# Four tokens instead of two side by side in the one-hot tiles of a product-key selection

## The reference

```
q   = (xt @ w_query).reshape(t, 8, 2, 128)
sc  = einsum('thpd,hpnd->thpn', q, sub_keys)
s1, i1 = top_k(sc[:, :, 0], 16);  s2, i2 = top_k(sc[:, :, 1], 16)
cand = s1[..., :, None] + s2[..., None, :]          # 16 x 16 candidates a head
top_s, ci = top_k(cand, 16)
experts = i1[ci // 16] * 128 + i2[ci % 16]          # 8 heads x 16 = 128 experts a token
gate = softmax(top_s)
act  = gelu(einsum('thkd,td->thk', u_tab[experts], xb))
y    = einsum('thk,thkd->td', gate * act, v_tab[experts])
```

## Time and profile before

| | value |
|---|---|
| median of three executions | 3107.72 us |
| profiled execution, its own time | 3113.7 us |
| its span, first to last instruction | 3111.9 us |
| TensorE busy over the span | 2840.0 us (91%) |
| VectorE busy | 2122.1 us (68%) |
| ScalarE busy | 1109.1 us (36%) |
| GpSimd busy | 1756.4 us (56%) |
| octets on the time axis | from 1344 to 1863 us |

### The profile page before, as it was taken

The page is one execution under the profiler, slowest core; times in us unless marked ns, Lnnn a source line. Parts: engine busy times, 40 slices in busy tenths (PEclk is TensorE's granted clock), DMA queues, the critical chain, the costliest instruction groups (busy, mean ns, idle before and its releaser), DMA issues. The chain is left out here.

```text
span 3111.9 us, 47231 instructions
## 1 busy us (share of the span) xinstructions
PE 2840.0 (91%) x15880; PEld 1549.7 (50%) x15880; DVE 2122.1 (68%) x3995; ACT 1109.1 (36%) x1480; POOL 1756.4 (56%) x1614
## 2 busy tenths in 40 slices
PE   6998788899999999988999999589999998999998
PEld 3444763455555555555666665334444443444443
DVE  2498974311667777767787874367778776877877
ACT  4332344122344444445666663212212221221212
POOL 1312553011244344455666667588888887888884
PEclk8999887999999999999999999899999999999999
DMA  3200002011233333357778777889999998999995
GB/s 114 77 24 21 0 30 113 28 40 40 80 112 113 108 116 106 118 200 262 281 274 296 269 285 272 268 314 359 338 365 352 342 366 289 341 350 364 331 353 225
DMA packets 260396, 648.60 MB, mean 208 GB/s; under 512 B 16992, under 2 KB 115552, under 8 KB 257136
## 3 DMA queue, kind: packets, MB, share of 16 engines
q1 hardware_dynamic: 186176, 378.33, 34.2%
q0 software_dynamic: 74160, 269.52, 23.5%
HBM read 542.39 MB, written 105.91 MB: 208 GB/s over the span
## 5 line engine op out<-in xcount | busy, mean ns | idle before, releaser
L91 POOL TENSOR_TENSOR w_low<-w_ring,w_high 128x1024 f16<-128x1024 f32 x164 | 385.6, 2352 | 976.6 <-ACT w_ring L86 976.5
L1247 PE MATMUL psum<-region_y,w_high 128*128 128x384 f16 x2048 | 675.5, 330 | 20.6 <-POOL w_low L91 19.0
L1667 PE MATMUL psum<-vh,wh 128*128 128x512 bf16 x1536 | 585.3, 381 | 100.0 <-POOL wl L1716 64.1
L1248 PE MATMUL psum<-region_y,w_high 128*128 128x384 f16 x2048 | 674.8, 329 | 0.0
L1249 PE MATMUL psum<-region_y,w_low 128*128 128x384 f16 x2048 | 674.3, 329 | 0.0
L1668 PE MATMUL psum<-vl,wh 128*128 128x512 bf16 x1536 | 585.1, 381 | 0.0
L1669 PE MATMUL psum<-vh,wl 128*128 128x512 bf16 x1536 | 584.4, 380 | 0.0
L1683 ACT ACTIVATE vh<-w_ring 128x1024 bf16<-128x1024 f32 x128 | 135.1, 1055 | 823.2 <-DMA w_ring<-in_v_t_dram 778.3
L1811 DVE TENSOR_TENSOR region_x<-region_x,psum 128x1024 f32<-128x1024 f32 x192 | 233.9, 1218 | 148.6 <-PE psum L1669 148.2
L1711 POOL TENSOR_TENSOR vl<-w_ring,vh 128x1024 bf16<-128x1024 f32 x128 | 273.3, 2136 | 49.5 <-ACT vh L1683 47.5
L1667 PEld LDWEIGHTS psum<-vh,wh 128*128 128x128 bf16 x1536 | 150.8, 98 | 298.6 <-issue 63.3
(11 more groups left out here) (236 smaller groups left out, 4882.4 us busy)
## 6 DMA issues: line engine op xcount, KB each, us to landing
w_ring<-in_u_t_dram SPq DMA_DIRECT2D x128, 512.0 KB, 4.1
w_ring<-in_v_t_dram SPq DMA_DIRECT2D x128, 512.0 KB, 6.6
acts_dram<-ge SPq DMA_DIRECT2D x128, 384.0 KB, 2.5
gates_dram<-scores SPq DMA_DIRECT2D x24, 2048.0 KB, 8.9
gt<-gates_dram SPq DMA_DIRECT2D x32, 1536.0 KB, 13.6
at<-acts_dram SPq DMA_DIRECT2D x32, 1536.0 KB, 21.1
w_ring<-in_w_stream_dram SPq DMA_DIRECT2D x20, 512.0 KB, 3.2
w_ring<-in_w_q_dram SPq DMA_DIRECT2D x16, 512.0 KB, 3.2
```

The lines of the kernel that those rows point to most:

```text
L91: pool.tensor_tensor(self.wl[:, s, :], self.wf[:, s, :], self.wh[:, s, :], ALU.subtract).then_inc(self.w_lo, 1)
L1247: pe.matmul(a, uh[:, par, row], xh[:, n, cols], start=(n == 0), stop=False)
L1248: pe.matmul(a, uh[:, par, row], xl[:, n, cols], start=False, stop=False)
L1667: pe.matmul(a, wh[:, par, c, rows], vh[:, par, c, cols], start=(c == 0), stop=False)
```

## The change

The tile `hot` gets another order of elements. Four tokens are neighbours instead of two, and two such groups make the octet instead of four pairs. The planes, the number of instructions, their sizes in elements, the waits and the buffers stay. VectorE still writes 1024 elements in one run, but reads its second operand in runs of four bf16 values (8 bytes) that repeat 128 times, instead of runs of two (4 bytes). The iota tile is 512 instead of 256 elements. TensorE reads the matrix of a token at every fourth bf16 value, a step of 8 bytes instead of 4, for the stationary and for the moving operand.

```diff
-    LANES = 2
     QUAD = OCT // 2
-    ROWS = OCT // LANES
@@
     hot = flat[...].bitcast(BF16).rearrange(
-        "p (r n q i t) -> p r n q i t", r=2, n=4, q=ROWS, i=P)
+        "p (r n q i t) -> p r n q i t", r=2, n=4, q=2, i=P)
@@
-    iota_2 = flat[:, at:at + P * LANES // 2].bitcast(BF16).rearrange("p (q i t) -> p q i t", q=1, t=LANES)
+    iota_4 = flat[:, at:at + P * QUAD // 2].bitcast(BF16).rearrange("p (q i t) -> p q i t", q=1, t=QUAD)
@@ octet on TensorE
-                        q, lane = divmod(QUAD * b + t, LANES)
                         for part in (2, 3):
-                            last = pe.matmul(psum[:, 4 + 2 * r + b, t * P:(t + 1) * P], hot[:, r, 0, q, :, lane],
-                                             hot[:, r, part, q, :, lane], start=(part == 2), stop=(part == 3))
+                            last = pe.matmul(psum[:, 4 + 2 * r + b, t * P:(t + 1) * P], hot[:, r, 0, b, :, t],
+                                             hot[:, r, part, b, :, t], start=(part == 2), stop=(part == 3))
@@ octet on VectorE
-                    return ap.rearrange("p (q a t) -> p q a t", q=ROWS, a=1).to_broadcast([P, ROWS, P, LANES])
-
-                iota = iota_2.to_broadcast([P, ROWS, P, LANES])
+                    return ap.rearrange("p (q a t) -> p q a t", q=2, a=1).to_broadcast([P, 2, P, QUAD])
+
+                iota = iota_4.to_broadcast([P, 2, P, QUAD])
@@ once, ahead of the octets
-            dve.tensor_copy(iota_2.rearrange("p q i t -> p (q i) t"), iota_x[:, :, 0:LANES])
+            dve.tensor_copy(iota_4.rearrange("p q i t -> p (q i) t"), iota_x[:, :, 0:QUAD])
```

## The result

The changed kernel takes 3144.35 us (median of four, 3141.85 to 3149.72), the kernel before beside it 3110.71 us (3107.39 to 3115.12): a ratio of 1.0102, 95% interval 1.0088 to 1.0116. It is 34 us slower. The forecast was 3154, its likeliest case 3135 to 3189.

The account below looks back on a forecast made before the run. TensorE was taken to pace the octets: 52.5 ns more a matmul makes 81 us over 96 octets, less 35 us absorbed by waits, so +46 on 3107.7 gives 3154 us. The 8-in-10 range was 3103 to 3185 us.

Parts of the forecast that it names:

- TensorE sets the pace of the stretch: Octets, slices 18 to 24: TensorE, busy 479.0 of 516.1 us, bounds the stretch from first to last octet.
- The 53 us, 41.6 of waits and 11 of low clock: Octets' stretch: 516 us less 463 of TensorE work leaves 53, waits for VectorE and matmuls at the lower clock.
- VectorE is not changed: VectorE's four octet instructions stay at 0.60 us each, as they already stream at twice the float32 rate.
- The rule weighed there: Skill's rule for VectorE: full rate only in runs of two or more adjacent 4-byte words, so 8-byte runs would gain.
- A matmul costs 110 ns: TensorE's octet matmuls at a step of 8 bytes: 110 ns instead of 57.5, 81 us over 96 octets.
- The bracket [57.5, 112] of the rows: Bounds in ns for an octet matmul: the 4-byte step's price below, float32 matmuls at full clock above.
- Two thirds of the waits absorb, 35 us: TensorE's waits and low clock in the octets, 53 us, take up 35 of the 81 us added.
- The sum: Whole kernel: 81 us more of TensorE less 35 absorbed gives +46 us, 3154 us from 3107.7.
- The step costs nothing: Rival on TensorE's octet reads: 8 bytes apart is still full rate, time 3108 us, give or take 4; chance 33%.
- A partial cost, because only one operand is slowed: Rival on TensorE's octet matmuls: 65 to 85 ns each, 3114 to 3129 us; chance 13%.
- faster: Rival on VectorE: 8-byte runs remove its fixed 0.06 us or some long instructions, 3098 us in the middle; chance 7%.
- would stay: Said under the rival of a slower VectorE (2%): stretched octet instructions, 2.62 us beside GpSimd's work, remain.

Follow-up runs that it names:

- lanes1: The kernel before with one token to a run: TensorE reads both operands contiguously, VectorE's second operand has inner step 0; 3248.8 us beside 3100.9.
- move32: The kernel before with the moving operand alone read at a step of 32 bytes instead of 4; 3387.7 us beside 3100.9.
- mov8: The kernel before with the moving operand's planes alone at a step of 8 bytes, the stationary one kept at 4; 3141.6 us, ratio 1.0088.
- rows_later_quad: The changed kernel with VectorE's two gathered rows of a slot taken one octet later; 3142.6 us, ratio 1.0110 to the kernel before.

## Why the prediction was right, point by point

- **TensorE sets the pace of the stretch.** Right; the stretch grew by 38 us, and nothing behind it took any back beyond what executions differ by.
- **The 53 us, 41.6 of waits and 11 of low clock.** The sum is right and its parts are not. The 41.6 us hold the wait of 4.73 us ahead of the first octet, which is no part of the stretch. Inside it TensorE idled 37 us (516.10 - 479.04), and the low clock had 16. The forecast uses only the 53, so it did not move.
- **VectorE is not changed.** Right: a median of 684 ns before and 683 after. The rule weighed there, by which it would have gained, finds nothing here to gain, and lanes1 shows that the limit lies between runs of one value and of two.
- **A matmul costs 110 ns.** Measured 116 to 118, so the term is 90 us and not 81. The bracket [57.5, 112] of the rows was passed slightly, and the step to it was loose: 9 to 10 bytes a ns make 102 to 114 ns, not 107 to 115. The way to it (9 to 10 bytes crossed in a ns) gave the right size from a wrong law, which is luck in part: up to 16 bytes the two laws give the same price, but at 32 bytes the engine crosses 17.7 bytes a ns (4096 in 231 ns). What it had right is that the step of 4 stands at the edge of what is free.
- **Two thirds of the waits absorb, 35 us.** This was the mis-sized term: 90 - 38 = 52 us, the whole of the 53 that the stretch had above 463. The prediction held back a part because TensorE would also delay its suppliers. It does (VectorE waits for it 83.5 us), but VectorE and the rows have 1.9 us a slot more, and TensorE waits for them nowhere in the stretch.
- **The sum.** +46 forecast, +34 timed. The errors, 9 us too little and 17 too much, partly cancel, and give 38 us, the growth of the stretch; the 4 us to the timed 34 are within what executions differ by.
- **The rivals.** "The step costs nothing" falls with the first octet, for the moving operand; it was right for the stationary one. "A partial cost, because only one operand is slowed" had the operand right and the rate wrong. For "faster" the long octet instructions did go, by their timing against GpSimd and not by the 8-byte runs (move32, with 4-byte runs, has none either); no time was gained by it, as TensorE sets the pace. That they "would stay", as the prediction had it under another rival, was wrong.

## What to carry to other kernels

A layout that is read across by TensorE as the moving operand should, by these runs on bf16, put at least four of its columns into each 16 bytes. That is a step of 4 bytes, and each step beyond costs in proportion up to 16. The stationary operand may be laid out more widely while its load is hidden behind matmuls: at 8 bytes it cost 2 to 3 us over 1536 of them. A cost that is added to the pacing engine first eats that engine's own waits, so weigh it against the stretch with its waits taken away: the 34 us seen here were 72 once another order of instructions had removed most of them.

## What was not expected of the hardware

- The clock fell in a TensorE that never idled. At steps of 16 and 32 bytes the granted clock was 0.90 over 807 and 804 us, at 8 bytes 1.00. No idle time in the profile points to it.
- A matmul that its moving operand's read paces takes as long at half the clock: 16 of them 1.85 us in mov8 at 0.50 granted and at 1.00, where at a step of 4 bytes they take 1.69 and 0.92.
- A slower matmul can leave the kernel no slower. With a step of 6 bytes TensorE has 96 x 0.47 = 45 us more to do, but the stretch took 507 us instead of 515 and the single run 3093.0 beside 3100.9. That is 96 x (3.90 + 1.39) = 508, the stretch without waits: TensorE was busy 506.7 of 508.7 us at a granted clock of 1.00. The run lies below every execution of the kernel before on record (the lowest 3098.4), but one run doesn't make it a gain.
- VectorE's octet instructions of up to 3.0 us appear beside GpSimd's line 91, in all 21 cases of the kernel before. They are absent (0.75 us at most) wherever the moving step is 8 bytes or more, with 8-byte runs on VectorE (the changed kernel, rows_later_quad) and with 4-byte runs (move32). The pace of TensorE decides which of VectorE's instructions meets line 91. No run takes line 91 away, so that it causes the stretching is argued from the overlap alone.
